# Residual and norms with tokens on partitions, 512-column products, in a three-block transformer kernel on one Trainium2 core

## What is computed

```python
c_act = silu(c)
for i in range(2):
    sh_a, sc_a, g_a, sh_f, sc_f, g_f = split(c_act @ ada_w[i] + ada_b[i], 6)
    h = rms_norm(x, norm_g[i, 0]) * (1 + sc_a) + sh_a
    y = moba_attention(h, ...) if i == 0 else diff_attention(h, ...)   # both end in o @ w_o
    x = x + g_a * rms_norm(y, norm_g[i, 1])
    h = rms_norm(x, norm_g[i, 2]) * (1 + sc_f) + sh_f
    x = x + g_f * rms_norm(swiglu(h, w_in[i], w_out[i]), norm_g[i, 3])
z = rms_norm(x, norm_mix_g);  x = x + concat(pool(z), lru(z) * gelu(z)) @ w_out
z = rms_norm(x, norm_mlp_g);  x = x + square(relu(z @ w_up)) @ w_down
z = rms_norm(x, norm_ple_g);  x = x + sigmoid(z @ w_gate + b) * (p @ w_proj)
out = rms_norm(x, norm_final_g)
```

## Time and profile before

| | us |
|---|---|
| median of 3 runs | 1074.29 |
| lowest, highest | 1073.21, 1080.11 |
| span of the profiled execution | 1076.4 |
| TensorE busy in it | 994.9 |
| VectorE busy in it | 690.4 |
| ScalarE busy in it | 507.4 |
| GpSimd busy in it | 51.3 |

### The profile page before, as it was taken

The page is one execution under the profiler, slowest core; times in us unless marked ns, Lnnn a source line. Parts: engine busy times, 40 slices in busy tenths (PEclk is TensorE's granted clock), DMA queues, the critical chain, the costliest instruction groups (busy, mean ns, idle before and its releaser), DMA issues.

```text
span 1076.4 us, 18734 instructions
## 1 busy us (share of the span) xinstructions
PE 994.9 (92%) x7732; PEld 956.7 (89%) x7732; DVE 690.4 (64%) x724; ACT 507.4 (47%) x609; POOL 51.3 (5%) x103
## 2 busy tenths in 40 slices
PE   1799997999999997999889999999899999999996
PEld 1699995999999986999869999999799899999996
DVE  4787865778668747688755444444697654554554
ACT  2455435444344355566654343344565544444464
POOL 3010001001000001000010000000100000000000
PEclk9999989999999998999989999999999999999998
DMA  9997862598779741754215554556135465556511
GB/s 334 354 317 273 313 217 91 196 312 276 257 272 325 256 139 57 237 183 149 91 67 169 183 195 163 188 193 205 61 132 182 124 190 193 164 188 194 171 65 40
DMA packets 128186, 207.67 MB, mean 193 GB/s; under 512 B 4498, under 2 KB 101907, under 8 KB 128147
## 3 DMA queue, kind: packets, MB, share of 16 engines
q1 hardware_dynamic: 116818, 163.59, 45.9%
q0 software_dynamic: 11328, 43.53, 11.7%
HBM read 206.04 MB, written 1.06 MB: 192 GB/s over the span
## 4 chain that ended last, share of the span: by engine, by line
PE 83%; DVE 6%; ACT 4%; issue 3%; DMA 3%; POOL 1%; SPq 0%; DVEq 0%; POOLq 0%; ACTq 0%
PE ps L501 25%; PE ps L502 25%; PE ps L503 25%; PE ps L563 4%; DMA raw<-in_moba_w_qkv 2%; DVE rstd L1208 1%; ACT w_hi L857 1%; DMA ada_raw<-in_ada_w 1%; PE ps L678 1%; PE ps L576 1%; PE ps L652 1%; POOL xt L474 1%; DVE ada_sum L1177 1%; DVE w_lo L1164 1%; DVE y L1227 1%
## 5 line engine op out<-in xcount | busy, mean ns | idle before, releaser
L1164 DVE TENSOR_TENSOR w_lo<-raw,w_hi 128x2048 fp32r<-128x2048 f32 x145 | 332.0, 2291 | 220.2 <-ACT w_hi L857 220.0
L501 PE MATMUL ps<-h_hi,w_hi 128*128 128x256 f32 x1376 | 397.3, 289 | 23.0 <-DVE h_lo L1222 12.8
L857 ACT ACTIVATE w_hi<-raw 128x2048 fp32r<-128x2048 f32 x145 | 276.7, 1910 | 267.4 <-PE ps L503 265.9
L502 PE MATMUL ps<-h_lo,w_hi 128*128 128x256 f32 x1376 | 392.7, 285 | 0.0
L503 PE MATMUL ps<-h_hi,w_lo 128*128 128x256 f32 x1376 | 392.4, 285 | 0.0
L501 PEld LDWEIGHTS ps<-h_hi,w_hi 128*128 128x128 f32 x1376 | 267.6, 194 | 27.4 <-issue 23.3
L502 PEld LDWEIGHTS ps<-h_lo,w_hi 128*128 128x128 f32 x1376 | 267.9, 195 | 0.3
L503 PEld LDWEIGHTS ps<-h_hi,w_lo 128*128 128x128 f32 x1376 | 267.5, 194 | 0.0
L501 PE MATMUL ps<-o_hi,w_hi 128*128 128x256 f32 x528 | 155.1, 294 | 5.5 <-DVE o_lo L1482 2.3
L502 PE MATMUL ps<-o_lo,w_hi 128*128 128x256 f32 x528 | 150.0, 284 | 0.0
L503 PE MATMUL ps<-o_hi,w_lo 128*128 128x256 f32 x528 | 149.9, 284 | 0.0
(11 more groups left out here) (227 smaller groups left out, 1063.2 us busy)
## 6 DMA issues: line engine op xcount, KB each, us to landing
raw<-in_ffn_w_in SPq DMA_DIRECT2D x44, 1024.0 KB, 5.2
ada_raw<-in_ada_w POOLq DMA_DIRECT2D x40, 1024.0 KB, 5.8
raw<-in_ffn_w_out SPq DMA_DIRECT2D x22, 1024.0 KB, 5.0
raw<-in_w_up SPq DMA_DIRECT2D x16, 1024.0 KB, 5.5
raw<-in_w_down SPq DMA_DIRECT2D x16, 1024.0 KB, 4.9
raw<-in_moba_w_qkv SPq DMA_DIRECT2D x12, 1024.0 KB, 7.3
raw<-in_diff_w_qkv SPq DMA_DIRECT2D x12, 1024.0 KB, 5.5
raw<-in_w_in SPq DMA_DIRECT2D x6, 1024.0 KB, 5.4
```

The costliest lines, as they stand in the source:

```text
L501: T.matmul(out_ap, hi_s, hi_m, start=start, stop=False, skip_group_check=True)
L502: T.matmul(out_ap, hi_s, lo_m, start=False, stop=False, skip_group_check=True)
L857: A.activation(w_hi[:, n.place], raw[:, n.place], ACT.Copy).then_inc(slab_hi, 1)
L1164: V.tensor_tensor(w_lo[:, n.place], raw[:, n.place], w_hi[:, n.place].bitcast(F32), ALU.subtract).then_inc(slab_lo, 1)
```

## The change

The residual and all that is added to it get tokens on partitions: `xt` is [128, 2 token tiles, 1024].

- Row slabs take the activations (128 tokens) as the stationary operand and move 512 columns of weights: 4 parts by 2 by 3 = 24 matmuls of 512 columns a slab (`row_part`). The four slabs of `w_gate` are loaded as halves of 512 columns and get the same form (`gate_part`).
- Sums of squares run along the free dimension: ScalarE squares 512 columns with `accum_out`, and root and reciprocal are of one column. The ones-matmuls of the norms, `add_y_pairs` on GpSimd and the interleaved sums are gone.
- For the next column slabs x is turned back: TensorE multiplies by `diag` (identity times the reciprocal) in layers 1 and 2 (`turn_scaled`, 4 float32 matmuls of 128 columns for each of 4 parts), or transposes plainly in the mixer block; VectorE applies gain and shift in `t_modulated` (four operations of 128 columns a part) or `t_plain` (one of 512).
- `post_norm` on VectorE and ScalarE is written out by token tile: the second tile's variance, update and turning come behind the first's. Column slab 0 waits for three of the four parts (`Z_NEED`), then for the fourth.
- The last two row slabs of each product run tile by tile (`row_last_two`): slab a tile 0, slab b tile 0, slab a tile 1, slab b tile 1. The second waits for the last chunk's `hid_lo` (or `o_ready`).
- The gates g_a and g_f are needed along the free dimension: `spread_row` (two float32 matmuls of 512 columns with ones) and `gate_row` on VectorE, with two DMAs of 0.5 MB each time. One-column reductions fall from 5 slots (80 records) to 2 (32), and four of the five reductions in layer 1's loop stay.
- Layer 2's heads: `attend` puts tokens on partitions (its probabilities become stationary, 6 matmuls of 128 columns for 4 of 256 and 128), four squares of 128 columns with `accum_out` follow on ScalarE, then a root and a reciprocal of 4 columns, a scaling on VectorE (`heads_normalised`), and TensorE turns the heads back (`turn_heads`), placed behind the v slab. `head_squares` is gone. VectorE's order in `pair` is as it was: `split_lo(n + 4)`, `biased`, `heads_normalised`.
- The split of the second slab after each norm moves behind the norm on ScalarE and VectorE; `clear_acc` moves behind the first two feed-forward slabs; the final norm scales x in place and stores four blocks.

```diff
 def pair(j, n, first):          # TensorE
     col_slab(n, 2 * l if first else None)
...
     scores(pairs * 3 + 2)
     if not first:
         attend(pairs)
+    v_slab(n + 2)
     if l and not first:
-        head_squares(j)
-    v_slab(n + 2)
+        turn_heads(j)
...
+def turn_heads(j):
+    pe.wait_ge(head_scaled, j)
+    o = hid[:].rearrange("p a b -> p (a b)")
+    for u in range(4):
+        last = T.transpose(ps[:, MISC, u * P:(u + 1) * P], o[:, u * P:(u + 1) * P], ident[:])
+    last.then_inc(head_turned, 1)
...
+def row_part(n, banks, parts, t, c, first, stop):
+    hi, lo = parts
+    wh, wl = as_rows(w_hi[:, n.place]), as_rows(w_lo[:, n.place])
+    for k in range(2):
+        last = three(ps[:, banks[2 * t + c]], hi[:, k, tokens(t)], lo[:, k, tokens(t)],
+                     wh[:, k, half(c)], wl[:, k, half(c)], first and k == 0, stop and k == 1)
+    return last
...
+def row_last_two(n, banks, parts, parts_next, wait_next):
+    pe.wait_ge(slab_lo, n.plus(2))
+    for t in range(ST):
+        for c in range(2):
+            last = row_part(n, banks, parts, t, c, False, False)
...
+        if t == 0:
+            wait_next()
+        for c in range(2):
+            last = row_part(n + 1, banks, parts_next, t, c, False, True)
...
+def turn_normed(z):
+    for t in range(ST):
+        pe.wait_ge(diag_ready, 2 * z + t + 1)
+        for c in range(2):
+            turn_scaled(z, t, c)
+        keep_warm(WARM[z], 8 if t == 0 else 10)
...
 def heads_out(pairs, j, at):    # ScalarE, layer 2
-    act.wait_ge(o_ready, pairs - 1)
-    A.activation(hid[:], ps[:, MISC], ACT.Copy)
-    A.activation(silu_g[:], ps[:, MISC], ACT.Square).then_inc(head_sq, 1)
+    for u in range(4):
+        last = A.activation(junk_x[:, 0, u * P:(u + 1) * P], ps[:, MISC, u * P:(u + 1) * P], ACT.Square,
+                            accum_out=hss[:, u:u + 1])
+    last.then_inc(head_sq, 1)
+    act.wait_ge(head_sq, j)
+    A.activation(hrms[:], hss[:], ACT.Sqrt, bias=eps[:, 0:1], scale=1.0 / HD).then_inc(head_rms, 1)
...
 def heads_normalised(j):        # VectorE
     dve.wait_ge(head_rms, j)
-    V.reciprocal(sq[:, 1], sq[:, 0]).then_inc(head_rstd, 1)
+    V.reciprocal(hrs[:], hrms[:]).then_inc(head_rstd, 1)
...
+def post_norm(b, banks, gains, gains_done, shift):   # VectorE
+    y_variance(b, 0)
+    y_gain(b, banks, 0, 0)
+    y_gain(b, banks, 0, 1)
+    y_inverse(b, 0)
+    x_update(b, 0)
+    x_inverse(z, 0)
+    y_variance(b, 1)
+    y_gain(b, banks, 1, 0)
+    turned_part(0)
+    y_gain(b, banks, 1, 1)
+    y_inverse(b, 1)
+    x_update(b, 1)
+    low_part(0)
+    x_inverse(z, 1)
+    turned_part(1)
+    turned_part(2)
+    low_part(1)
+    low_part(2)
+    turned_part(3)
+    low_part(3)
```

## The result

The changed kernel takes 1058.88 us (median of 4 runs, 1056.67 to 1063.82) against 1076.98 of the kernel before in the same comparison (four runs, 1073.21 to 1080.11): ratio 0.9834, 95% interval 0.9809 to 0.986. Its profiled span is 1057.0 us against 1076.4, so 19.4 us were saved where 40.6 were forecast. The time lies above the forecast's range, which ended at 1056.

What follows compares the result with a forecast made beforehand. TensorE was taken to bound the kernel inside stages, and the chain ending in VectorE's h_lo between them. Seven terms summed to -40.6 us, span 1076.4 to 1035.8, median 2.1 lower: 1034 us; range 1007 to 1056.

Steps and rivals of the forecast that it cites:

- Term 1: All 55 row and gate slabs: 1320 products of 512 columns at 0.216 us for two narrow at 0.120, -31.7 us.
- The rival at 0.227: Wide products cost 0.227 us each from a fixed toll of 0.013 on a product; 1048 us, chance 0.2.
- Terms 2 and 4: Output projections without squares cutting the last slab, -9.1 us; TensorE's new wait for layer 2's heads, three pairs, +21.3 us.
- its rival: Layer 2's pairs: `turn_heads` finds its heads ready, a pair takes 21.6 us; 1007 us, chance 0.15.
- Term 3: Gaps at the three full norms: first product 10.3 us after the last one, -22.0 us.
- Terms 5 and 6: Conditioning with `spread_row` in both feed-forward networks, +0.9 us; shorter entry into the mixer block, -6.3 us.
- Term 7: Other new waits: `hid_lo` between last row slabs, `w_out`, the end with its gate parts, the start; +6.3 us.
- the likeliest case: Whole kernel with wide products at 0.216 us and layer 2's wait: 1024 to 1044 us, chance 0.52.

Runs made afterwards that it cites:

- the series: Changed kernel with eight, then ten more, series of 48 independent products behind TensorE's last slab; starts 0.227 and 0.2285 us apart for float32r, 512 by 128.
- the run that removed it: Changed kernel with VectorE's order in layer 2's pairs made heads' scaling, biased scores, then split: 1037.67 us, ratio 0.9635 to the kernel before.
- the kernel with all changes: Changed kernel with heads-scores-split order, later splits, four waits removed, zeros before the mixer block only, layer 2's second projection slab earlier: 1017.09 us, ratio 0.9442.
- the run with zeros: Changed kernel with products of zeros between and behind the turnings in front of the mixer block and the MLP: 1064.21 us, ratio 0.9865.
- the run with the first series: Changed kernel with eight series of 48 independent products behind TensorE's last slab; float32r starts 0.227 us apart for 512 columns, 0.120 for 256.

## Why the forecast was wrong

Measured from landmark to landmark of TensorE (the first product of a stage) in the two profiled executions, in us. What the wide products save, 24 x 0.012 = 0.288 a slab, is taken out of each stretch and stands in the first row, 55 x 0.288; the run with narrow products gives 15.9 for the same. The rows are rounded, the sum is that of the spans.

| term | forecast | measured | off by |
|---|---|---|---|
| 1, wide products | -31.7 | -15.8 | +15.9 |
| 2 and 4, projections and layer 2's heads | +12.2 | +10.8 | -1.4 |
| 3, full norms | -22.0 | -23.1 | -1.1 |
| 5 and 6, networks and entry to the mixer block | -5.4 | -1.0 | +4.4 |
| 7, the other new waits | +6.3 | +9.9 | +3.6 |
| sum | -40.6 | -19.4 | +21.2 |

- **Term 1** is the step that failed, with three quarters of the miss. The forecast took 0.216 because at half clock the product has no toll, and concluded that the toll is gone once the array is busy some 213 ns. The first half is right for the wide product too (0.427 at half clock). The conclusion isn't: at full clock the toll is 14 ns at 213 ns of array time as at 107. What frees a product of the toll is the clock, not its length. The rival at 0.227 had the right price, the reading "a fixed toll on a product, 0.013" that it came from is what the series show, and it was given 0.2. The Trainium skill, page "TensorE: Matmul & The Clock Gate", section "Back-to-back issue gap", gives by its formula for the isolated gap at full clock 216 ns for this product and 109 for the narrow one. In bfloat16 the series agree with both (0.216 and 0.109), in float32r with neither (0.228 and 0.120).
- **Terms 2 and 4** held. The wait is 6.2 us for 6.8, released by VectorE's `hid`, three times. The half clock behind it took 1.7, 2.1 and 2.4 us where 2.2 each was taken. The whole was +21.3 in the forecast, and came at 20.5: +18.1 in the pairs and 2.4 of half clock in the projection's first slab. The 20.8 us of the run that removed it are another quantity, counted against pairs that never wait (21.6) and less what that run lost in the projection; between these two cases the forecast has 27.1 us (21.3 and the 5.8 of its rival), the runs 24.0 in the pairs and the same 2.4. The projections came out at 32.0 and 29.6 for 31.0 and 26.5 plus the half clock, with 1.2 each for the width.
- **Term 3** held. Gaps of 10.46, 10.47 and 11.68 stand against 10.3. Behind them the clock was full, and 5.5 us were gained there for 3.2 forecast. A third of this hangs on token-tile order: in the kernel with all changes plain order gave 7.7 us back at the three norms.
- **Terms 5 and 6.** The waits for `hid_lo` came as forecast (2.25 for 2.3), but the half clock behind the two in the networks, 1.7 us each, was not in the sum, nor were the 2.1 us of it in the first slab of the mixer block (7.91 for 5.8); these 5.5 us are more than the miss of 4.4. The forecast charged new idle time with half clock in layer 2's pairs only.
- **Term 7.** `w_out`'s gap (+2.85 for +3.0) and the MLP (+2.0 for +2.3) held. One wait was missed: `row_last_two` waits for both slabs' splits before it starts, although it reads the second one 12 products later, 1.5 us in `w_out`. The two waits in the gate slabs were in the sum, at 3.1 and 4.7, and came at 2.7 and 3.1, but the 24 products behind the one took 1.7 us more than at 0.228 and the 48 behind the other 1.6. The end was +2.4 for +0.5.
- **Slips in the sum.** The parts of term 2's first projection add to 30.6, not 31.0, those of the end to 45.2, not 46.2; some others are 0.1 off. None of this is near the size of the miss.
- That the likeliest case and its nearest rival were both inside the range and the time was not comes from adding them: 0.227 alone gives 1048, and the missed waits and half clocks of 4.4 + 3.6 us lie on the same side and fill the 8 us that the range had for the gaps. The last 3.7 us are the step from span to time: the forecast put the median 2.1 below the span, as three runs of the kernel before had it, and for the changed kernel it came out 1.9 above. (Of one and the same execution the time is 1.7 above the span.) With the forecast's step the span of 1057.0 gives 1054.9, just inside. So the place outside the range hangs on which execution was profiled; the 15.9 us of term 1 don't.

## What to carry to other kernels

Before counting a gain of wider products, take the cost of one product at full clock from two widths, or take the fixed toll as it stands: a price read at half clock can't be carried over. A new wait of TensorE can cost more than its length. Of the five waits of 2.2 to 3.1 us in the changed kernel's networks, MLP and gate slabs, four were followed by a loss of 1.6 to 1.7 us at half clock and one by 0.1; three of 6.2 us were followed by 1.7 to 2.4, and three of 1.0 to 1.5, in front of second slabs and in `w_out`, by nothing. So the longer waits in a sum need that surcharge. And when a step is placed on one engine, the order of the engine that feeds it has to be moved with it: two moves on VectorE were worth more (20.8 us) than all 1320 wide products (15.9), and token-tile order turned from a loss of 4.5 us into a gain of 8.1 once the splits stood behind what TensorE waited for.

## What the hardware showed beside that

- A float32r product of 128 by 128 by 128 starts 0.112 us behind the one before, hardly less than one of 256 moving columns (0.120). With 64 or 32 stationary columns it takes 0.060.
- A stationary tile used again costs the same as a new one (0.227 us for 512 columns either way).
- The same code had spells of half clock of different length in different executions. The last two row slabs of the first projection, 48 products, took 12.64 us in the changed kernel, 13.76 in the run with zeros and 11.03, at full clock throughout, in the run with the first series. The place isn't random, though: in twelve of the thirteen traces here (the kernel before among them) the clock fell inside, or at most 1.3 us behind, the one-column products that stand just before (32 of them, 149.65 to 153.14 in the changed kernel), without a pause. No run takes these products away, so that they cause it isn't shown. Differences of 2 us between two profiled executions say little; the medians and the local windows carry the conclusions above.
